# Gathering tokens already transposed, in a mixture-of-experts loop on one core

## The reference

```python
gates = jnp.einsum('tk,tke->te', top_w, jax.nn.one_hot(top_i, N_EXPERTS))
def expert(acc, xs):                     # 32 experts, D_MODEL = D_FF = 1024
    wgu, bgu, wd, bd, g = xs
    u = tok @ wgu + bgu                  # tok: 288 tokens x 1024
    glu = jnp.minimum(u[:, ::2], 7.0); lin = jnp.clip(u[:, 1::2], -7.0, 7.0)
    a = glu * jax.nn.sigmoid(1.702 * glu) * (lin + 1.0)
    return acc + g[:, None] * (a @ wd + bd), None
```

## Time and profile before

| | us |
|---|---|
| median of 3 runs | 1337.11 |
| lowest and highest | 1335.3, 1340.05 |
| the profiled execution | 1335.3 |
| its span, first to last instruction | 1333.5 |
| PE busy in it | 1240.2 (93%) |
| ScalarE, VectorE busy | 270.7 (20%), 302.0 (23%) |

### The profile page before, as it was taken

How to read it: one execution, slowest core, us unless ns; L and a number is a source line. 1 busy time by engine, 2 the same in 40 slices (tenths; PEclk the granted TensorE clock), 3 DMA queues, 4 the chain that set the end, 5 groups by cost and what they waited for, 6 DMA issues and landing times.

```text
span 1333.5 us, 19209 instructions
## 1 busy us (share of the span) xinstructions
PE 1240.2 (93%) x7314; PEld 526.2 (39%) x7314; DVE 302.0 (23%) x549; ACT 270.7 (20%) x581; POOL 65.7 (5%) x80
## 2 busy tenths in 40 slices
PE   7999998999789999999999999999999999999996
PEld 4588744454433333333333333333333333333332
DVE  1144535125321111122111111211111112111113
ACT  3144341112411120212112020211212020211102
POOL 2021003322000000000000000000000000000000
PEclk9999999999799999999999999999999999999999
DMA  9489977987969999999999999999999999999961
GB/s 347 170 312 357 341 269 275 347 298 246 389 288 402 415 430 425 431 427 430 428 422 430 427 427 427 427 425 428 422 423 427 425 430 425 424 423 425 429 288 37
DMA packets 76877, 500.55 MB, mean 375 GB/s; under 512 B 8873, under 2 KB 9026, under 8 KB 52258
## 3 DMA queue, kind: packets, MB, share of 16 engines
q1 hardware_dynamic: 73314, 488.04, 89.8%
q0 software_dynamic: 3520, 11.93, 2.6%
HBM read 495.22 MB, written 4.72 MB: 375 GB/s over the span
## 4 chain that ended last, share of the span: by engine, by line
PE 81%; DVE 6%; issue 4%; DMA 3%; ACT 3%; SPq 2%; POOL 0%; DVEq 0%; ACTq 0%; POOLq 0%
PE psum L873 33%; PE psum L900 17%; PE psum L428 7%; PE psum L415 5%; PE psum L806 5%; PE psum L864 2%; PE psum L833 2%; ACT arena L960 2%; SPq L390 2%; PE psum L514 2%; DMA arena<-cache_v 1%; PE psum L821 1%; PE psum L810 1%; DMA arena<-x_sample 1%; DMA arena<-cache_k 1%
## 5 line engine op out<-in xcount | busy, mean ns | idle before, releaser
L873 PE MATMUL psum<-arena 128*64 128x512 f32 x2048 | 448.2, 596 | 0.0
L873 PEld LDWEIGHTS psum<-arena 128*64 128x64 f32 x2048 | 145.3, 137 | 300.8 <-issue 300.8
L900 PE MATMUL psum<-arena 128*64 128x512 f32 x1024 | 231.8, 600 | 23.2 <-issue 11.7
L960 ACT ACTIVATE arena<-psum 128x512 f32<-128x512 f32 (+4 forms) x250 | 138.2, 576 | 459.0 <-PE psum L900 145.8
L1534 DVE TENSOR_SCALAR arena<-psum 128x512 f32<-128x512 f32 x32 | 22.1, 691 | 662.0 <-PE psum L873 662.0
L900 PEld LDWEIGHTS psum<-arena 128*64 128x64 f32 x1024 | 73.9, 137 | 147.7 <-issue 137.9
L1159 ACT ACTIVATE arena<-arena 128x512 f32<-128x512 f32 x32 | 20.2, 630 | 446.8 <-DVE arena L1534 446.8
L428 PE MATMUL psum<-arena 128*128 128x512 f32 x224 | 101.9, 613 | 1.6 <-ACT arena L960 1.6
L415 PE MATMUL psum<-arena 128*128 128x128 f32 (+1 forms) x692 | 86.9, 278 | 8.6 <-ACT arena L960 5.4
L833 PE MATMUL psum<-arena 128*128 128x512 f32 x128 | 63.5, 618 | 24.5 <-DVE arena L1557 24.5
L415 PEld LDWEIGHTS psum<-arena 128*128 128x128 f32 (+1 forms) x692 | 75.5, 144 | 22.9 <-issue 10.8
(11 more groups left out here) (210 smaller groups left out, 650.0 us busy)
## 6 DMA issues: line engine op xcount, KB each, us to landing
arena<-w_gate_up SPq DMA_DIRECT2D x128, 2048.0 KB, 10.6
arena<-w_down SPq DMA_DIRECT2D x64, 2048.0 KB, 14.2
arena<-cache_v SPq DMA_DIRECT2D x128, 256.0 KB, 5.2
arena<-cache_k SPq DMA_DIRECT2D x96, 256.0 KB, 5.7
arena<-w_in SPq DMA_DIRECT2D x7, 2048.0 KB, 10.1
arena<-cache_k POOLq DMA_DIRECT2D x32, 256.0 KB, 5.7
arena<-w_out SPq DMA_DIRECT2D x2, 2048.0 KB, 10.1
out<-arena POOLq DMA_DIRECT2D x1, 2048.0 KB, 13.3
```

The source lines that it names most:

```text
L873: last = mm(psum[64 * g:64 * (g + 1), b, :], xt[:, 2 * kk + m, lhs], gate_slot[slot][:, m, c:c + 512], start=False, stop=kk == 3 and m == ...
L900: last = mm(psum[64 * g:64 * (g + 1), 2, :], at_sb[:, m, SLOTS * q:SLOTS * (q + 1)], down_slot[slot][:, m, 512 * g:512 * (g + 1)], start=q ...
L960: return nc.scalar.activation(out, in_, ACT.Copy, scale=scale)
```

## The change

`gather` makes the transposed result at once. Now `hn` is stationary (128 feature columns at a time, every second column of a stretch of 256) and `sel` moves (128 columns). For each of the eight feature blocks three matmuls add up in their 128 columns of bank 6 or 7. The copy to `xg_sb`, the eight transposes and the semaphores between them go.

```diff
             def gather(n):

                 pe.wait_ge(sel_ready, n + 1)
-                for tile in range(2):
-                    for half in range(2):
-                        mm(psum[:, 6 + half, :], sel[:, tile].rearrange("p a b -> p (a b)"),
-                           hn[:, tile, 512 * half:512 * (half + 1)], start=tile == 0, stop=False)
-                for half in range(2):
-                    rows = slice(NS * half, NS * (half + 1))
-                    last = mm(psum[:, 6 + half, :], sel[rows, 2].rearrange("p a b -> p (a b)"),
-                              hn[rows, 2, 512 * half:512 * (half + 1)], start=False, stop=True)
-                last.then_inc(xg_full, 1)
-
-            def turn_x(n):
-
-                pe.wait_ge(xg_ready, n + 1)
                 for kk in range(2):
                     for m in range(2):
-                        for half in range(2):
-                            cols = slice(512 * half + 256 * kk + m, 512 * half + 256 * (kk + 1), 2)
-                            last = tr(psum[:, 6 + half, P * (2 * kk + m):P * (2 * kk + m + 1)],
-                                      xg_sb[:, cols], ident)
+                        for bank in range(2):
+                            cols = slice(512 * bank + 256 * kk + m, 512 * bank + 256 * (kk + 1), 2)
+                            o = psum[:, 6 + bank, P * (2 * kk + m):P * (2 * kk + m + 1)]
+                            for tile in range(2):
+                                mm(o, hn[:, tile, cols], sel[:, tile].rearrange("p a b -> p (a b)"),
+                                   start=tile == 0, stop=False, skip_group_check=True)
+                        for bank in range(2):
+                            cols = slice(512 * bank + 256 * kk + m, 512 * bank + 256 * (kk + 1), 2)
+                            o = psum[:, 6 + bank, P * (2 * kk + m):P * (2 * kk + m + 1)]
+                            rows = slice(NS * bank, NS * (bank + 1))
+                            last = mm(o, hn[rows, 2, cols], sel[rows, 2].rearrange("p a b -> p (a b)"),
+                                      start=False, stop=True, skip_group_check=True)
                 last.then_inc(xt_full, 1)
...
-                        if ahead and e == 1 and q == 0:
-                            turn_x(n + 1)
 
             pe.wait_ge(hn_copied, 1)
             gather(0)
-            turn_x(0)
...
             def gathered(n):
-                act.wait_ge(xg_full, n + 1)
-                copy(xg_sb, psum[:, 6:8, :].rearrange("p a b -> p (a b)")).then_inc(xg_ready, 1)
                 act.wait_ge(xt_full, n + 1)
```

More of the change, by code:

```diff
@@ L291, in build_kernel @@
         work_i = at(Q + 2430, 2, EXTRA).bitcast(I32)
-        xg_sb = at(Q + 1242, D)
         pair_of = at(Q + 2466, 64)
@@ L364, in build_kernel @@
             "sel_ready", "selg_ready", "xt_full", "xt_ready"))
-        picked_ready, xg_full, xg_ready = map(sem, ("picked_ready", "xg_full", "xg_ready"))
+        picked_ready = sem("picked_ready")
         sq_ready, f_rstd, yo_ready, stored = map(sem, ("sq_ready", "f_rstd", "yo_ready", "stored"))
@@ L940, in _ @@
                     gather(n)
-                    turn_x(n)
                     pair(n, in_extra(n), False)
```

## The result

Over 20 executions of each, the changed kernel took 1344.17 us (1340.48 to 1348.16) and the kernel before 1336.01 us. The ratio is 1.0059, with a 95% interval from 1.0045 to 1.0073. It is slower by about 8 us; the forecast was +2.9 us, 1340.0, with a range from 1334 to 1355. The profiled execution took 1345.02 us and has a span of 1343.2 us, 9.7 us more than before.

A forecast was written before the change was run, and what follows sets the result against it. PE's own order of work was taken to bound the kernel. Fifteen pairs at +0.28 us gave +4.2, the start -1.3, so +2.9 on 1337.1: 1340.0 us, own range 1336.5 to 1345, 8 in 10 within 1334 to 1355.

The forecast's parts named there:

- DMA has a reserve: In the loop, weight parts land early enough to leave some 25 us before transfers would hold PE.
- What goes, 6.00 us: Per pair on PE: the old gather, 4.69 us, and the transposes with their shape changes, 1.31 us, disappear.
- what comes, 6.28 us: Per pair on PE: the new gather's four groups, each 1.16 us of 128-row passes plus 0.41 us of 32-row matmuls.
- double load: Rival: a matmul's strided load in the gather costs double; +40 us, 1377; chance 0.08.
- matmuls not side by side: Rival: each group's two 32-row matmuls do not overlap at 128 columns; 0.9 us a pair, 13 us, 1353; chance 0.08.
- The 0.73 us before L900: PE idle stretch in the pair, read as PE waiting for ScalarE's copy of the activation.
- plain rate: Rival: the gather's strided load costs no more than an adjacent one; -0.04 us a pair, -1.9 us, 1335.2; chance 0.14.
- The start, -1.3 us: Once, ahead of the loop: the new first gather ends at about 367.9 us, 1.3 us earlier than before.
- two groups are done by 364.7 and two at full speed need 3.1 us: First gather: two groups at half clock, 2.3 us each, until 364.7, then two at full clock.
- I let it stay and keep 1.7 us on both sides: Half-clock stretch from 375.0 to 378.4 us, costing 1.7 us: assumed unchanged, with 1.7 us uncertainty either way.
- the 0.05 for something not seen: Chance 0.05 of a slower result from a wait or clock stretch that the prediction had not seen.
- Hidden loads: Rival: PE hides the gather's loads and shape changes; -1.6 us a pair, -25 us with the start, 1312; chance 0.08.

The follow-up runs named there:

- unbroken first gather: Changed kernel, but the gather ahead of the loop runs its sixteen 128-row matmuls first, then its eight 32-row ones; 1338.32 us, ratio 1.0029.
- filler: Changed kernel plus five 512-column matmuls, result unread, behind the last router matmuls ahead of the first gather; 1343.92 us, ratio 1.0067.

## Why the prediction was right or wrong

- **PE bounds the loop, DMA has a reserve.** Right. PE waits for no part in the loop in any trace, and a pair under the transfers' time was still paid in full (58.18 us, 15 x 0.9 = 13 us of the gain).
- **What goes, 6.00 us; what comes, 6.28 us.** Right, 6.29 measured. Reading the group off L821 and L810 gave all its parts, the two small matmuls side by side included. The rivals of a double load and of matmuls not side by side fall. Two smaller readings were off. The loads of L809 were to last 200 to 260 ns and last 193 to 197. The 0.73 us before L900 was put down to ScalarE, where the row says issue; it is there in the changed kernel too.
- **The plain rate and the page of the Trainium skill.** "SBUF — State Buffer", section "Door 1: The DMA port swizzle", has a step of two fp32 values as free. The run with adjacent columns does not agree for a matmul's load: 59.37 against 59.11 us a pair. That the plain rate would bring the pair back to before, -0.04 forecast, is +0.04 measured (59.11 against 59.07).
- **The start, -1.3 us.** Here the prediction failed, in the step "two groups are done by 364.7 and two at full speed need 3.1 us", which took the clock's return at 364.7 as given, and in "I let it stay and keep 1.7 us on both sides". In the kernel before, the clock came back while L806's 512-column passes ran; the new gather puts alternating groups there, and it does not come back. In the profiled execution the start came out 5.1 us worse than forecast: +3.8 us. Part of that is a size: a group at half clock takes 2.7 us, not 2.3, since its two changes of shape cost more than 0.1 each, and with the clock back at 364.7 that alone would have been about 0.4 us (1.7 groups done by then, 2.3 left at 1.57 us, the end at 368.3 in place of 367.9). Whether the start gains 1.3 us without the clock's part is not shown; the kernel with the old pairs allows it. I treated the granted clock as a property of the place in time; it depended on the instructions that the change replaced.
- **The sum.** +2.9 forecast, +8.2 measured between the medians. The loop's +4.5 is read from the traces. With the start's -1 it would give +3.5. The rest, 4.7 us, is put down to the clock by argument: the time at half clock rose by 16 us (51.1 against 35.0), worth 6.4 us at 0.4 a us and 3.2 at the changed kernel's own 0.2, which makes 9.9 or 6.7 in all. Two runs bear on it and do not agree. The unbroken first gather, measured beside the changed kernel on one chip, took 5.0 us off, 3.3 to 4 of them beyond its own shorter length; the old first gather had 11.5 us of the half clock back and was no faster. So the clock's share stays open. That 1344.2 lies inside the range of 1336.5 to 1345 is in part luck: the range allowed 1.7 us for the clock, and the long stretch had only a share of the 0.05 for something not seen.
- **"Hidden loads".** A group takes 1.57 us where this rival wanted under 1.45, so it falls. The way to that side was to have fewer changes of shape, which the prediction priced and did not follow up. It said 0.1 each, but its own rows hold 0.2: L821's 1.16 us less 8 x 0.12, for one change from start to start, as the six that went away confirm. The group's sum was right because it took the rows whole.

## What to carry to other kernels

Swapping the operands of a matmul to save a transpose keeps the streamed columns but multiplies the loads and the changes of array shape; count both, and group the matmuls of one shape (here -1.19 us of 6.29 per gather, and -1.2% in place of +0.6%). Where a bank then holds several open sums, only the first matmul in it may carry the start. When a change replaces the work under which the clock came back, price that stretch at both clock levels, not at the one in the trace.

## What the runs showed of the hardware

- 128-row groups of 8 passes that alternate with 32-row pairs, 10.9 us of them, left the granted clock at 0.50 in every trace that had them ahead of the loop without a filler (four of four such traces: the changed kernel twice, with old pairs, with adjacent columns, each 27.3 us). The same matmuls sorted by shape had it back after 10.2 or 13.7 us. Behind a filler it came back under the alternating groups too, after 6.8 us. In the pairs the same gather runs between dense work, and the clock stays at 1.00.
- A load with a step of two fp32 values lasts 4 ns longer than an adjacent one (196 against 192), yet 8 passes take 1.14 us against 1.09 from the start of L809 to the start of L815, and a group 1.57 against 1.51. Four groups make 0.24 of the pair's 0.26 us.
- A start in one block of a PSUM bank, with other blocks of the bank still open, costs their sums and no time: the two kernels that differ in it have the same 58.18 us pair. The Trainium skill, "PSUM — Partial Sum Buffer", section "The four PSUM rules", states that such a start clears the marks of the whole bank, so that the next sum overwrites; the lost sums agree.
